# One transformer layer with retrieved experts in fp32: gates of the branches moved into the softmax pause, output projection by tiles, one-hot scaling on ScalarE

## The chip, the cores and the metric

The kernel runs on one core of one Trainium2 chip. The metric is the device time of one execution in microseconds (us). In the profile PE is TensorE's matmul, PEld its weight load, DVE is VectorE, ACT is ScalarE, POOL is GpSimd and SP is SyncE, which here only issues transfers. L740 is line 740 of the kernel before.

## What is computed

One layer on 512 tokens of width 1024, all in fp32. First half: a combined projection of x feeds a sliding-window attention (8 query heads, 2 key heads, chunks of 64 tokens, window of 2 chunks, sink logits) and a gated linear recurrence (4 heads, states of 128 x 128, chunks of 64). The two branches are projected to the width, weighted by sigmoid gates and sent through one output projection; then comes a layer norm. Second half: each token picks 128 of 16384 experts.

```python
mixed = (sigmoid(ga) * (attn @ w_proj_attn) + sigmoid(gh) * (rec @ w_proj_hgrn))
x = layer_norm(ALPHA * x + mixed @ w_out, ln1_g, ln1_b)
# peer_ffn: top 16 of 128 keys twice per head, top 16 of their sums, softmax g
hid = einsum('thkd,td->thk', u[e], xt)
act = gelu(hid)
out = einsum('thk,thkd->td', g * act, v[e])
x = layer_norm(ALPHA * x + out, ln2_g, ln2_b)
```

## The kernel before, in words

**Tiles.** The tokens are four tiles of 128. The first half of the layer runs twice: front A has tile 0, front B ("the big front") tiles 1 to 3, with six chunks. In the second half tiles 0 and 1 are GATHERED: GpSimd fetches single rows of u and v with indirect transfers (L1592), 512 KB for one expert slot of 128 tokens, into 12 slots. VectorE reduces each u row against x (L1163, rows 0 to 127 for tile 0 and 256 to 383 for tile 1) and adds each v row to an accumulator (L1178, rows 128 to 255 and 384 to 511). Tiles 2 and 3 are DENSE: TensorE computes the hidden values of all 16384 experts in 128 chunks (`hidden(c)`, L835), and ScalarE applies gelu (L1054). 96 of the chunks come first, the last 32 alternate with `combine(i)` (L860), which multiplies by v. The gates of the dense tiles are built as a matrix: VectorE compares indices with an iota (L1484) and scales the second half by the gate (L1486), four tokens at a time (a quad, 64 of them, two buffers). TensorE multiplies the two one-hots (`spread(q)`, L853), ScalarE copies the product (`copy_gates`, L1073), and every 8 quads it is stored to memory.

**Order.** Each engine's program is written out by hand and all waits are semaphores. VectorE's program is woven from the front's steps and the gathered rows: `rows_until(q)` works off rows until q of the 512 are done, and the positions stand in constants (AT_STATE, AT_REC, AT_MIX and so on). `rows_until(at_mix(m))` stands ahead of mix m: 90 rows for m = 0, then 95, 106, 111 and so on up to 143. In the output projection it stands ahead of the first three blocks of columns (152, 161, 170), then come EARLY_ROWS = 204, the routing of tiles 1, 2 and 3 with 7 or 8 rows each part, and `rows_until(2 * NE)`, 256, ahead of the one-hots. HOT_ROWS are spread over the quads.

**Front B on TensorE.** Projections of the features (L575) and of seven token items (L587, the first five early), scores, then the softmax. `turn_weights(c)` (L637) and `times_v(c)` (L652 to L659) make the attention of chunk c, L677 and L682 the recurrence's operands, `chunk_kv` (L696) and `tile_out` (L707, L711) its states and outputs. Then come four pairs of `gates(m), gates(m+1), branches(m), branches(m+1)` (L740, L750, L752). gates(m) for m >= 2 waits for mix m - 2, since it uses its banks. The output projection (L775) has 12 units of one tile and 256 columns, in four banks. VectorE takes each unit (L1343) and norms a tile after its last one (L1352 to L1363). The normed tiles are turned (L788) and projected to queries (L815).

**ScalarE in front B.** Exponentials of the softmax (L968), copies of the token items (L913), scaling of the softmax (L976), copies of the turned weights (L983) and of the attention (L991), kendT (L995), the recurrence's output (L1000), roots (L1003), recT (L1008), gate sigmoids (L1014). A function of another table is preceded by an ACT_TABLE_LOAD.

**Queues.** SP issues all loads in program order: weight items of 1 MB through a ring of three slots, each waiting for the item that its slot held; later u and v chunks. In the spread phase the loads of hidden weights run four chunks ahead, and the first gates are loaded behind the one for chunk 99. GpSimd's queue holds the gathers and, at its end, the stores of tiles 0 and 1.

```python
            for c in range(FIRST):
                if c == TURN_AT:
                    picks(0)
                    picks(1)
                if c == SPREAD_AT:
                    pe.wait_ge(pick_out, 2 * len(DENSE))
                hidden(c)
                for q in range(quads_by(c - 1), quads_by(c)):
                    spread(q)
```

Of the kernel before, what the change touches and what calls it, by code (L numbers as in the profile page):

```python
# [12 lines left out]
P = 128  # L13
# [34 lines left out]
RING, ITEMW = 3, 2048  # L48
# [29 lines left out]
EXP_AT = 49  # L78
TURN_AT = 51
SPREAD_AT, SPREAD_END = 52, 82  # L80
# [3 lines left out]
EARLY_ROWS, PAIR_ROWS, HALF_ROWS = 204, 7, 8  # L84
HOT_ROWS = 30
MID_ROWS = 314
# [4 lines left out]
ODD_STEP, AT_OUT, OUT_STEP, HGRN_STEP, STATE_STEP = 5, 152, 9, 3, 2  # L91
# [91 lines left out]
def build(nc, x, xT, w_items, keysT, pos, inv_freq, sinks, lb_logits, norm_g,  # L183
          ln1, ln2, ident_d, causal_d, chunk_d, iota_d, u_rows, v_rows, u_cols, v_cols, gates_d, act_d, out):
    with ExitStack() as ctx:
# [25 lines left out]
        ring = view(64, RING, ITEMW)  # L211
# [90 lines left out]
        hot_ready = sem("hot_ready")  # L302
        g_done = sem("g_done")
# [14 lines left out]
        out_done = [sem(f"out_done{k}") for k in range(2)]  # L318
# [36 lines left out]
        B.sig = view(152, 2, 2, B.n)  # L355
# [81 lines left out]
        def _(sp):  # L437
# [115 lines left out]
            for k in range(2):  # L553
                sp.wait_ge(out_done[k], 32)

        @block.tensor
        def _(pe):
# [3 lines left out]
            def front(F, other=None):  # L561
# [99 lines left out]

                pe.wait_ge(F.reached, V_ZERO)
# [60 lines left out]
                pe.wait_ge(F.proj_out, 2 * N_HQF + N_TOK * nt)  # L723
# [6 lines left out]

                def gates(m):
                    k = I_MIX + 3 * (m // 2) + m % 2
                    item_in(pe, F, k)
                    w = item(F, k).rearrange("p (c n) -> p c n", n=P)
                    if m >= 2:
                        pe.wait_ge(F.mix_out, m - 1)
                    b = 4 * (m % 2)
                    for g in range(2):
                        for c in range(KC):
                            last = mm(bank[:, b + g, 0:n], w[:, g * KC + c, :], F.act_in[:, c, :],  # L740
                                      start=c == 0, stop=c == KC - 1)
                    last.then_inc(F.gate_done, 1)
# [917 lines left out]
```

## Time and profile before

| | |
|---|---|
| median of 3 runs | 1645.16 us (1645.09 to 1646.64) |
| the profiled execution | 1645.0 us, its span 1643.2 us |
| mean granted TensorE clock | 0.964 |
| TensorE matmul busy | 1543.6 us, 94% |
| VectorE busy | 1131.2 us, 69% |
| ScalarE busy | 270.4 us, 16% |
| moved by transfers | 532.38 MB, mean 324 GB/s |

The times of the rows are counted from the start of the span. A busy TensorE is not TensorE at its peak: the ends of its matmuls are modelled. An fp32 matmul stands as two records, so a unit of 8 matmuls is "x16". A group's span in the timeline overlaps the next one's by the length of a matmul; the distance between two starts is the pace.

### The profile page before, as it was taken

To read this page: it belongs to the slowest core of one execution; us is meant where nothing else is said; L and a number is where in the kernel's file an instruction comes from. 1 tells how busy PE (TensorE), PEld (TensorE's weight loads), DVE (VectorE), ACT (ScalarE), POOL (GpSimd) and SP (SyncE) were. 2 spreads that over 40 slices of the span, in tenths; PEclk is the share of its full clock that TensorE was granted. 3 is DMA by queue.
4 is the path that set the end of the run, shared out by engine and by line. 5 is a ranking of instruction groups with operands and counts; after the bars stand their busy time and mean duration, and the time that the engine had idled before them with its cause. 6 is when DMAs were issued, how large, how long until landed. Compare 5 with 4: busy or idle time off the path is not lost.

```text
span 1643.2 us, 17974 instructions
## 1 busy us (share of the span) xinstructions
PE 1543.6 (94%) x6542; PEld 1098.7 (67%) x6542; DVE 1131.2 (69%) x2364; ACT 270.4 (16%) x543; POOL 610.0 (37%) x518
## 2 busy tenths in 40 slices
PE   8798999789998799999999999889999999999997
PEld 7697778665557566888888888756666544444443
DVE  1413899978769999999979999366556735545523
ACT  2601213621010111111134453100000000000000
POOL 0000543466667463322322223465534633424100
PEclk9898998779999799999999999989999999999999
DMA  7586967777999797998978878999999999999962
GB/s 297 203 275 212 397 228 265 251 246 273 412 398 374 275 403 282 316 330 288 327 255 312 319 277 299 410 383 405 404 408 406 405 402 380 395 393 392 369 218 77
DMA packets 145511, 532.38 MB, mean 324 GB/s; under 512 B 14864, under 2 KB 34064, under 8 KB 133904
## 3 DMA queue, kind: packets, MB, share of 16 engines
q0 software_dynamic: 74016, 269.52, 43.7%
q1 hardware_dynamic: 70256, 244.94, 40.0%
q10 hardware_dynamic: 1152, 16.78, 2.6%
q8 instruction: 52, 0.85, 0.2%
q14 instruction: 35, 0.29, 0.0%
HBM read 503.92 MB, written 27.26 MB: 323 GB/s over the span
## 4 chain that ended last, share of the span: by engine, by line
PE 74%; DVE 12%; DMA 7%; issue 3%; ACT 2%; POOL 0%; SPq 0%; DVEq 0%
PE bank L835 26%; PE bank L860 22%; PE bank L740 7%; PE bank L815 6%; PE bank L853 3%; DMA arena<-v_cols_d 3%; DVE arena L1163 2%; DMA arena<-gates_d 2%; DVE arena L1178 2%; PE bank L775 2%; PE bank L750 2%; PE bank L752 2%; PE bank L587 1%; PE bank L575 1%; DMA arena<-u_cols_d 1%
## 5 line engine op out<-in xcount | busy, mean ns | idle before, releaser
L1592 POOL DMA_INDIRECT arena<-u_d,arena x256 | 319.7, 1249 | 566.4 <-DVE arena L1163 315.9
L860 PE MATMUL bank<-arena 128*128 128x512 f32 x1024 | 448.2, 595 | 16.8 <-DVE arena L1501 14.1
L835 PE MATMUL bank<-arena 128*128 128x256 f32 x2048 | 452.9, 379 | 4.0 <-DMA arena<-u_cols_d 4.0
L835 PEld LDWEIGHTS bank<-arena 128*128 128x128 f32 x2048 | 386.6, 190 | 69.4 <-issue 17.8
L1592 POOL DMA_INDIRECT arena<-v_d,arena x256 | 288.9, 1129 | 362.9 <-DVE arena L1178 287.2
L860 PEld LDWEIGHTS bank<-arena 128*128 128x128 f32 x1024 | 195.1, 191 | 250.7 <-issue 227.2
L1178 DVE SCALAR_TENSOR_TENSOR arena<-arena 128x1024 f32<-128x1024 f32 x256 | 327.9, 1281 | 42.4 <-DMA arena<-v_d,arena 32.2
L1163 DVE CUSTOM_DVE_ANT_0 arena<-arena 128x1024 f32<-128x1024 f32 x256 | 304.2, 1221 | 68.5 <-DMA arena<-u_d,arena 67.9
L1501 DVE TENSOR_TENSOR arena<-arena 128x256 f32<-128x256 f32 x128 | 52.9, 420 | 159.5 <-DMA arena<-act_d 103.1
L1054 ACT ACTIVATE arena<-bank 128x256 f32<-128x256 f32 x128 | 49.2, 384 | 491.2 <-PE bank L835 491.1
L815 PE MATMUL bank<-arena 128*128 128x128 f32 (+1 forms) x512 | 118.9, 394 | 1.4 <-ACT arena L1021 1.4
L740 PE MATMUL bank<-arena 128*128 128x128 f32 (+1 forms) x512 | 113.9, 384 | 0.0
L815 PEld LDWEIGHTS bank<-arena 128*128 128x128 f32 x512 | 81.0, 200 | 35.8 <-issue 2.6
L587 PE MATMUL bank<-arena 128*128 128x256 f32 x448 | 100.0, 385 | 2.5 <-ACT arena L913 2.5
L740 PEld LDWEIGHTS bank<-arena 128*128 128x128 f32 x512 | 78.1, 192 | 34.8 <-issue 1.6
L587 PEld LDWEIGHTS bank<-arena 128*128 128x128 f32 x448 | 86.3, 193 | 15.5 <-ACT arena L913 2.9
L853 PE MATMUL bank<-arena 128*128 128x128 f32 x512 | 64.7, 278 | 5.5 <-DVE arena L1486 4.3
L1073 ACT ACTIVATE arena<-bank 128x512 f32<-128x512 f32 x64 | 65.3, 1083 | 21.9 <-PE bank L853 20.9
L853 PEld LDWEIGHTS bank<-arena 128*128 128x128 f32 x512 | 63.1, 191 | 8.6 <-DVE arena L1486 6.8
L775 PE MATMUL bank<-arena 128*128 128x256 f32 x256 | 60.4, 401 | 8.3 <-DVE arena L1333 5.9
L575 PE MATMUL bank<-arena 128*128 128x128 f32 (+1 forms) x256 | 58.5, 395 | 7.2 <-DMA arena<-w_items_d 7.2
L775 PEld LDWEIGHTS bank<-arena 128*128 128x128 f32 x256 | 51.5, 203 | 17.2 <-DVE arena L1333 6.7
(200 smaller groups left out, 1035.6 us busy)
## 6 DMA issues: line engine op xcount, KB each, us to landing
arena<-w_items_d SPq DMA_DIRECT2D x66, 1024.0 KB, 7.2
arena<-u_cols_d SPq DMA_DIRECT2D x128, 512.0 KB, 6.6
arena<-v_cols_d SPq DMA_DIRECT2D x128, 512.0 KB, 8.9
gates_d<-arena ACTq DMA_DIRECT2D x8, 2048.0 KB, 8.2
arena<-gates_d SPq DMA_DIRECT2D x16, 1024.0 KB, 16.7
act_d<-arena SPq DMA_DIRECT2D x8, 1024.0 KB, 9.3
arena<-act_d SPq DMA_DIRECT2D x8, 1024.0 KB, 16.7
arena<-u_d,arena POOLq DMA_INDIRECT x256, 8.7
```

Of the source, the lines that this page charges most:

```text
L575: last = mm(bank[:, b % 4, 0:n], w[:, c, b % 2 * P:(b % 2 + 1) * P], F.act_in[:, c, :], start=c == 0, stop=c == KC - 1)
L587: last = mm(bank[:, b % 4, 0:TW], F.act_in[:, c, t * P:(t + 1) * P], w[:, c, :], start=c == 0, stop=c == KC - 1)
L740: last = mm(bank[:, b + g, 0:n], w[:, g * KC + c, :], F.act_in[:, c, :], start=c == 0, stop=c == KC - 1)
L775: last = mm(bank[:, u % 4, 0:TW], F.mixT[:, c, t * P:(t + 1) * P], w[:, c, :], start=c == 0, stop=c == KC - 1)
L815: last = mm(bank[:, b % 4, 0:n], w[:, c, half * P:(half + 1) * P], F.act_in[:, c, :], start=c == 0, stop=c == KC - 1)
L835: last = mm(bank[:, 4 + c % 2, 0:ND], u_buf[:, c % UBUFS, k, :], B.act_in[:, k, B.n - ND:B.n], start=k == 0, stop=k == KC - 1)
L853: last = mm(bank[:, 6 + q % 2, j * NK:(j + 1) * NK], hot[:, q % 2, j, :], hot[:, q % 2, QUAD + j, :], start=True, stop=True)
L860: last = mm(bank[:, 2 * n + half, :], act_slot(i)[:, n * P:(n + 1) * P], v_buf[i % VBUFS][:, half * 512:(half + 1) * 512], start=i == 0, s ...
L1073: fn(stage[g % 2][:, :, k * QUAD:(k + 1) * QUAD].rearrange("p e t -> p t e"), bank[:, 6 + q % 2, :].rearrange("p (t e) -> p t e", t=QUAD), ...
L1163: v.tensor_tensor_reduce(rows[:, s, :], rows[:, s, :], x1[:, t, :], 1.0, 0.0, ALU.mult, ALU.add, hid[:, k:k + 1]).then_inc(row_used, 1)
L1178: v.scalar_tensor_tensor(out=acc[t], in0=rows[:, s, :], scalar=wv[:, k:k + 1], in1=acc[t], op0=ALU.mult, op1=ALU.add).then_inc(row_used, 1)
L1592: pool.indirect_dma_start(rows[:, r % SLOTS, :], None, table, bass.IndirectOffsetOnAxis(eidx[:, t, k:k + 1], 0)).then_inc(landed[r % SLOTS ...
```

## The change

Seven edits come together.

- **Gates in the pause.** In front B gates(0) and gates(1) are issued after the last token item, around the first two `turn_weights`, into banks 0 to 3 instead of 0, 1, 4, 5. Their sigmoids come on ScalarE after the kendT copies, and chunk_kv(0) waits for all four. B.sig gets a place of its own. ScalarE copies the last token item ahead of the softmax scaling.
- **Early part of the projection.** Six of the eight matmuls of units 0 and 1 are issued ahead of the last mix, in both fronts.
- **Units by tiles.** The order of units is tile by tile; VectorE's rows within the projection are only those up to 152.
- **Ring** of four slots.
- **One-hots.** The scaling by the gate goes from VectorE (one multiply per quad) to ScalarE (four activations of 128x128), ahead of the gelu of the same chunk, with a semaphore hot_scaled.
- **copy_gates** writes in the order of the stage and reads the bank with a stride.
- **Positions.** Everything at the picks and the spread is one chunk later; row quotas change. The stores of the gathered tiles are on SP's queue.

```diff
-RING, ITEMW = 3, 2048
+RING, ITEMW = 4, 2048
-EXP_AT = 49
-TURN_AT = 51
-SPREAD_AT, SPREAD_END = 52, 82
+EXP_AT = 50
+TURN_AT = 52
+SPREAD_AT, SPREAD_END = 53, 83
-EARLY_ROWS, PAIR_ROWS, HALF_ROWS = 204, 7, 8
-HOT_ROWS = 30
-MID_ROWS = 314
+EARLY_ROWS, PAIR_ROWS, HALF_ROWS = 184, 7, 7
+HOT_ROWS = 52
+MID_ROWS = 316
-        B.sig = view(152, 2, 2, B.n)
+        B.sig = view(48, 2, 2, B.n)
 def out_units(F):
-            return ([(k, t) for k in range(N_OUT - 2) for t in range(F.nt)]
-                    + [(k, t) for t in range(F.nt) for k in range(N_OUT - 2, N_OUT)])
+            return [(k, t) for t in range(F.nt) for k in range(N_OUT)]
+        def gate_bank(F, m):
+            return 2 * m if F is B and m < 2 else 4 * (m % 2)
 # SP, at the end
-            for n, t in enumerate(DENSE):
-                sp.wait_ge(y2_ready, len(GATHERED) + n + 1)
-                sp.dma_start(out[t * P:(t + 1) * P, :], x1[:, t, :]).then_inc(out_done[1], 16)
+            for n, t in enumerate(GATHERED + DENSE):
+                sp.wait_ge(y2_ready, n + 1)
+                sp.dma_start(out[t * P:(t + 1) * P, :], acc[t] if t in GATHERED else x1[:, t, :]).then_inc(out_done, 16)
 # TensorE
+                if F is B:
+                    gates(0)
                 pe.wait_ge(F.reached, V_ZERO)
                 turn_weights(0)
+                turn_weights(1)
+                if F is B:
+                    gates(1)
                 for c in range(F.nc):
-                    if c + 1 < F.nc:
+                    if 0 < c < F.nc - 1:
                         turn_weights(c + 1)
                     times_v(c)
...
-                pe.wait_ge(F.proj_out, 2 * N_HQF + N_TOK * nt)
+                if F is B:
+                    pe.wait_ge(F.gate_ready, 4)
+                else:
+                    pe.wait_ge(F.proj_out, 2 * N_HQF + N_TOK * nt)
                 chunk_kv(0)
...
+                pe.wait_ge(F.gate_ready, 2 * KC - 2)
+                pe.wait_ge(F.mix_out, KC - 2)
+                for u in range(2):
+                    item_in(pe, F, I_OUT + u)
+                    for c in range(KC - 2):
+                        sum_out(u, c)
                 pe.wait_ge(F.mix_out, KC)
...
 def spread(q):
-                pe.wait_ge(hot_ready, q + 1)
+                pe.wait_ge(hot_scaled, q + 1)
 # ScalarE
+                if F is B:
+                    for k in range(TOK_EARLY + 1, N_TOK):
+                        copy_tok(k)
                 for c in range(F.nc):
                     act.wait_ge(F.soft_den, c // (F.nc // 2) + 1)
...
-                for k in range(TOK_EARLY + 1, N_TOK):
-                    copy_tok(k)
+                if F is A:
+                    for k in range(TOK_EARLY + 1, N_TOK):
+                        copy_tok(k)
...
+                if F is B:
+                    gate_sigmoids(0)
+                    gate_sigmoids(1)
                 for t in range(nt):
                     act.wait_ge(F.o_done, t + 1)
...
+            def scale_hots(q):
+                act.wait_ge(hot_ready, q + 1)
+                for j in range(QUAD):
+                    d, t = divmod(q * QUAD + j, P)
+                    one = hot[:, q % 2, QUAD + j, :]
+                    last = fn(one, one, ACT.Copy, scale=gT[d][:, t:t + 1])
+                last.then_inc(hot_scaled, 1)
 def copy_gates(q):
-                fn(stage[g % 2][:, :, k * QUAD:(k + 1) * QUAD].rearrange("p e t -> p t e"),
-                   bank[:, 6 + q % 2, :].rearrange("p (t e) -> p t e", t=QUAD), ACT.Copy).then_inc(g_out, 1)
+                fn(stage[g % 2][:, :, k * QUAD:(k + 1) * QUAD],
+                   bank[:, 6 + q % 2, :].rearrange("p (t e) -> p e t", t=QUAD), ACT.Copy).then_inc(g_out, 1)
...
+                for q in range(quads_by(c - 1), quads_by(c)):
+                    scale_hots(q)
                 gelu(c)
                 for q in range(quads_by(c - 1), quads_by(c)):
                     copy_gates(q)
 # VectorE
-                    if t == 0 and k < N_OUT - 1:
-                        rows_until(AT_OUT + OUT_STEP * k)
+                    if u == 0:
+                        rows_until(AT_OUT)
...
-                    steps(lambda: v.tensor_tensor(out, iota..., idxT..., ALU.is_equal))
-                    v.tensor_tensor(out[:, 1, :, :], out[:, 1, :, :],
-                                    gT[d][:, ts]..., ALU.mult).then_inc(hot_ready, 1)
+                    v.tensor_tensor(out, iota..., idxT..., ALU.is_equal).then_inc(hot_ready, 1)
 # GpSimd, at the end
-            for t in GATHERED:
-                pool.wait_ge(y2_ready, t + 1)
-                pool.dma_start(out[t * P:(t + 1) * P, :], acc[t]).then_inc(out_done[0], 16)
```

## Rows read from the trace of the kernel before

**Rows 1.** The page's first part: busy us of each engine, share, instructions.
```profile
PE 1543.6 (94%) x6542; PEld 1098.7 (67%) x6542; DVE 1131.2 (69%) x2364; ACT 270.4 (16%) x543; POOL 610.0 (37%) x518
```

**Rows 2.** TensorE's waits: total us, times, longest.
```profile
PE bank L775 <- DVE arena L1333: 5.9, 2, 4.9
PE bank L853 <- DVE arena L1486: 4.3, 5, 1.2
```

**Rows 3.** Two stretches: length, busy us of each engine, granted clock, DMA share, GB/s.
```profile
320.00:334.00 14.00, 7.71 (x83) 6.12 (x85) 13.64 (x28) 10.67 (x30) 6.47 (x4) 0.53 0.71 246
840.00:1015.00 175.00, 169.55 (x1025) 154.91 (x1024) 156.94 (x195) 81.03 (x103) 39.31 (x29) 1.00 0.79 287
```

**Rows 4.** Timeline of TensorE, 300 to 345 us: start, length, line, [idle before].
```profile
310.02 7.17 PE L587 MATMUL bank<-arena 128*128 128x256 f32 x32 [2.53 <-ACT arena L913]
...
328.38 0.49 PE L656 MATMUL bank<-arena 128*64 128x64 f32 x4 [6.29 <-ACT arena L983]
...
342.64 1.71 PE L696 MATMUL bank<-arena 64*128 64x128 f32 x16
```

**Rows 5.** Timeline of ScalarE, 318 to 345 us.
```profile
318.47 7.12 ACT L976 ACTIVATE arena<-arena,mx 128x128 f32<-128x128 f32 x24 [3.77 <-DVE mx L1271]
325.61 1.28 ACT L913 ACT_TABLE_LOAD   x1
326.90 0.94 ACT L913 ACTIVATE arena<-bank 128x256 f32<-128x256 f32 x3
...
341.85 0.60 ACT L995 ACTIVATE arena<-bank 128x512 f32<-128x512 f32 x1 [0.73 <-PE bank L677]
```

**Rows 6.** The chain that ended last, the gate groups: start, us, what.
```profile
368.26 22.10 PE bank L740 x64
...
403.80 20.64 PE bank L740 x64
```

**Rows 7.** Timeline of VectorE, 375 to 400 us: first and last of 14 rows.
```profile
375.08 1.22 DVE L1163 CUSTOM_DVE_ANT_0 arena<-arena 128x1024 f32<-128x1024 f32 x1
...
389.98 1.22 DVE L1163 CUSTOM_DVE_ANT_0 arena<-arena 128x1024 f32<-128x1024 f32 x1
...
398.75 1.02 DVE L1331 TENSOR_TENSOR arena<-arena,bank 128x384 f32<-128x384 f32 x2 [7.54 <-PE bank L752]
```

**Rows 8.** Timeline of TensorE, 500 to 565 us.
```profile
501.57 37.61 PE L775 MATMUL bank<-arena 128*128 128x256 f32 x160 [4.89 <-DVE arena L1333]
...
563.03 13.39 PE L815 MATMUL bank<-arena 128*128 128x384 f32 x32 [0.69 <-ACT arena L1021]
```

**Rows 9.** Timeline of VectorE, 500 to 610 us: rows, a norm's start and the next tile's units.
```profile
501.43 12.39 DVE L1178 SCALAR_TENSOR_TENSOR arena<-arena 128x1024 f32<-128x1024 f32 x9
...
541.78 1.29 DVE L1352 BATCH_NORM_STATS2 stats<-arena 128x6 f32<-128x512 f32 x2
...
547.46 0.75 DVE L1343 SCALAR_TENSOR_TENSOR arena<-arena,bank 128x256 f32<-128x256 f32 x2
...
560.36 47.13 DVE L1178 SCALAR_TENSOR_TENSOR arena<-arena 128x1024 f32<-128x1024 f32 x34
```

**Rows 10.** Timeline of VectorE, 837 to 844 us: end of the picks, first quad.
```profile
837.61 0.29 DVE L1462 TENSOR_TENSOR arena<-arena 128x128 f32<-128x128 f32 x1
841.83 1.23 DVE L1484 TENSOR_TENSOR arena<-iota,chunk_mask 128x1024 f32<-128x1024 f32 x1 [3.93 <-ACT chunk_mask L1065]
843.09 0.69 DVE L1486 TENSOR_TENSOR arena<-arena,chunk_mask 128x512 f32<-128x512 f32 x1
```

**Rows 11.** Timeline of 848 to 854 us, TensorE and ScalarE: one chunk with two quads.
```profile
848.29 1.95 PE L853 MATMUL bank<-arena 128*128 128x128 f32 x16
849.38 1.99 ACT L1073 ACTIVATE arena<-bank 128x512 f32<-128x512 f32 x2 [0.51 <-PE bank L853]
850.07 3.62 PE L835 MATMUL bank<-arena 128*128 128x256 f32 x16
853.53 2.02 PE L853 MATMUL bank<-arena 128*128 128x128 f32 x16
```

More of the change, by code:

```diff
@@ L302, in build @@
         hot_ready = sem("hot_ready")
+        hot_scaled = sem("hot_scaled")
         g_done = sem("g_done")
@@ L317, in build @@
         y2_ready = sem("y2_ready")
-        out_done = [sem(f"out_done{k}") for k in range(2)]
+        out_done = sem("out_done")
         A.tok = view(0, 1, TOKW)
@@ L660, in times_v, with gates @@
                     last.then_inc(F.av_done, 1)
+                def gates(m):
+                    k = I_MIX + 3 * (m // 2) + m % 2
+                    item_in(pe, F, k)
+                    w = item(F, k).rearrange("p (c n) -> p c n", n=P)
+                    if m >= 2:
+                        pe.wait_ge(F.mix_out, m - 1)
+                    elif F is B:
+                        pe.wait_ge(F.proj_out, 2 * N_HQF + N_TOK * nt)
+                    b = gate_bank(F, m)
+                    for g in range(2):
+                        for c in range(KC):
+                            last = mm(bank[:, b + g, 0:n], w[:, g * KC + c, :], F.act_in[:, c, :],
+                                      start=c == 0, stop=c == KC - 1)
+                    last.then_inc(F.gate_done, 1)
+                if F is B:
+                    gates(0)
                 pe.wait_ge(F.reached, V_ZERO)
                 turn_weights(0)
+                turn_weights(1)
+                if F is B:
+                    gates(1)
                 for c in range(F.nc):
-                    if c + 1 < F.nc:
+                    if 0 < c < F.nc - 1:
                         turn_weights(c + 1)
@@ L728, in front @@
                     chunk_kv(2 * t + 2)
[L731 to L742, printed above, removed]
                 def branches(m):
@@ L770, in front @@
                     item_in(pe, F, I_OUT + k)
-                    w = item(F, I_OUT + k).rearrange("p (c n) -> p c n", c=KC)
                     if u >= 4:
                         pe.wait_ge(F.y_out, u - 3)
-                    for c in range(KC):
-                        last = mm(bank[:, u % 4, 0:TW], F.mixT[:, c, t * P:(t + 1) * P], w[:, c, :],
-                                  start=c == 0, stop=c == KC - 1)
+                    for c in range(KC - 2 if u < 2 else 0, KC):
+                        last = sum_out(u, c)
                     last.then_inc(F.y_done, 1)
@@ L996, in front, with gate_sigmoids @@
                        ACT.Copy).then_inc(F.kend_out, 1)
+                def gate_sigmoids(m):
+                    act.wait_ge(F.gate_done, m + 1)
+                    if m >= 2:
+                        act.wait_ge(F.mix_out, m - 1)
+                    for k in range(2):
+                        fn(F.sig[:, m % 2, k, :], bank[:, gate_bank(F, m) + k, 0:n], ACT.Sigmoid).then_inc(F.gate_ready, 1)
+                if F is B:
+                    gate_sigmoids(0)
+                    gate_sigmoids(1)
                 for t in range(nt):
@@ L1009, in front @@
                                ACT.Copy).then_inc(F.rec_out, 1)
[L1010 to L1014 removed]
+                    if m >= 2 or F is A:
+                        gate_sigmoids(m)
                     if F is B and m == GELU_M:
```

28 lines of the change are left out of this document (14 added, 14 removed).

## The prediction

> **What bounds the kernel now.** I read the page's first part, then the waits of TensorE, then the timelines of the stretches that the edits touch, engine by engine. TensorE is busy for 1543.6 of 1643.2 us [rows 1]: nearly all of the time is its matmuls, which the change neither adds nor removes, so it can only win some of the 100 us in which TensorE idles, or lose more. The waits [rows 2] show where edits can bite: the output projection waits for the last mix (L775, 5.9 us in two waits, one per front, the longest 4.9), and the spread for the one-hots (L853, 4.3 in five waits). The longest wait of all, that of the first combination of the dense part for its gates, the change doesn't reach: the gates are requested only behind the weight loads that wait for hidden(95), so the stall moves with the end of the spread phase. Behind TensorE stands VectorE: 156.9 of 175 us busy in the spread stage, ScalarE 81.0 [rows 3]. From 560.4 us to the first one-hot VectorE waits for almost nothing: it is as dense as TensorE.
>
> The profiled execution took 1645.0 us, its span 1643.2, the median of the runs 1645.16; the sum goes by 1645.0, and as the two agree within 0.2 us it stands for the median too. A difference of 0.2%, 3.3 us, is about what a measurement of this kernel can tell from none.
>
> **1. Front A.** Its projection begins six of eight summands of two units before the last mix. The wait it covers is the other L775 wait, 5.9 - 4.9 = 1.0 us [rows 2]. **-1.0**. A's new order of units is the old one (one tile), and its gates don't move.
>
> **2. Gates in the pause (front B).** TensorE finishes the last token item at 317.2, turns two chunks, and starts times_v at 328.4 [rows 4]. It idles since ScalarE scales until 325.6, loads a table and copies the last item's three tiles [rows 5]. The copies now come before the scaling; the last tile's can be done at about 317.7, and the scaling, which waits for VectorE until 318.5, isn't moved. One item of gates is half of 20.64 us, 10.3 [rows 6]. So gates(0) runs 317.7 to 328.1 and is hidden. Then two turns (1.1 at full clock) and gates(1), 10.3: times_v(0) starts at 339.5, not 328.4. The six chunks took 10.1 us from 328.4 to 338.5, partly at the half clock (0.53 granted over 320 to 334 [rows 3]); the odd and even chunks that ran at full clock give some 7.7 us for six, since TensorE now comes from dense work. They end at 347.2: +8.7. The turns and copies of the recurrence follow as before (ScalarE's last copy 342.45, now 351.2 [rows 5]). Here a wait is added: chunk_kv(0) needs the banks, so the four gate sigmoids: a table load and 4 x 0.44 us. The load took 1.29 us from the end of the scaling to the next activation [rows 5]. So 351.2 + 1.3 + 1.75 = 354.2, against 342.6 [rows 4]: **+11.6** for everything behind, VectorE's states and norms included. A low clock over chunk_kv adds about 1 (between 0 and 2): +12.6. The Trainium skill (ScalarE: Activation LUTs, What ACT_TABLE_LOAD costs) gives about 2.66 us for a switch of tables, its drain included; the row above shows 1.29, so the row decides, and by the page the wait would be 1.4 us longer.
>
> What is gained behind: 22.10 us of gates at 368.3 go [rows 6], so TensorE could start the branches soon after the norms. But gates(2) waits for mix(0), and VectorE owes 14 gathered rows ahead of it, whatever TensorE does: they ran from 375.1 to 391.1, 1.147 us each, and VectorE then waited 7.5 us for the branches [rows 7]. That slack of 7.5 us, and the 3.5 us between mix(0)'s end (400.3) and gates(2), are all that the delay can use up. The rows now end at 391.1 + 12.6 = 403.7, mix(0) takes 1.6, and gates(2) starts at 405.3, where it started at 403.8 [rows 6]: **+1.5**. TensorE idles some 5 us ahead of it and may find the half clock: between 0 and 3 us (half of a 6 us stretch), taken as **+1.6**. So 20 us of moved gates give nothing here: what is late next is VectorE's row quota, which isn't changed. The later pairs take TensorE 31 us, VectorE 16 rows and two mixes, 23 us, so they stay bound by TensorE.
>
> **3. Projection of front B.** Before: last mix done 501.5, matmuls 501.6 to 550, third norm's result at 560.3, query projection 563.0 [rows 8, 9]. After, with the same start: 24 of the records run in the 4.9 us wait; the first four units are done at about 510.2 (3.46 us each at full clock). VectorE does its nine rows until 513.8 [rows 9], so the fifth unit waits for a bank until 514.2. Eight units take 27.7: 541.9. VectorE finishes the first and second tile under these (1.5 us for four units, 5.7 for a norm [rows 9]); the third tile's norm ends at 541.9 + 0.4 + 5.9 = 548.2, against 560.3: -12.2. A half clock after the 4 us gap would cost up to 2.4; I take **-11.2**.
>
> The sum at this point: -1.0 + 1.5 + 1.6 - 11.2 = **-9.1**, for TensorE and VectorE alike.
>
> **4. From there to the spread.** Here the lead doesn't carry. VectorE did rows 152 to 170 within the projection; now it waits there. Before the first one-hot it had done 264 rows, now 256: the constants say 240, but rows_until(256) still stands ahead of the one-hots. From the third norm that is 104 rows of the second kind, instead of 86 of those and 8 of the first: +18 x 1.386 [rows 9] - 8 x 1.147 [rows 7] = +15.8. The picks used to be ready at 837.9 and the first one-hot waited 3.9 us for their way through TensorE and ScalarE [rows 10]; now 16 rows cover that way. First one-hot: 837.9 - 9.1 + 15.8 + 0.1 = 844.7, not 841.8. Then 1.3 for the comparison and 1.3 for ScalarE's four scalings (7.12 / 24 = 0.297 each [rows 5], plus start) instead of VectorE's 0.69 [rows 10]. The first spread starts at 847.4, against 848.3 [rows 11]: -0.9. TensorE has by then done one hidden chunk more (3.46): **-4.4** instead of -9.1. It waits some 4 us for the first pair of one-hots.
>
> **5. The spread phase.** Sixty-four quads in 30 chunks: 26 chunks with two, 4 with three. With two quads a chunk takes 3.46 + 1.8 = 5.26 us [rows 11]. ScalarE needs 0.38 + 2 x (1.19 + copy). The copy took 1.0 to 1.08 us where a plain 128x512 copy takes 0.60 [rows 11, 5]; its write now goes in runs of four words, its read from the bank is strided instead. At 0.6 ScalarE needs 4.0 us, at 1.08 4.9: under 5.26, so no stall. The removed multiplies (64 x 0.69 = 44 us) are VectorE's, which waited for TensorE here anyway: nothing. With three quads, the third one-hot waits for the first spread (two buffers). Before, the two spreads of 1.8 were followed by a stall of at most 1.2 [rows 2, 11]: its spread started some 3.1 us after the chunk's end. Now the chain is spread 0.9, comparison 1.3, scaling 1.3, and only then the gelu 0.35 and the copy of the first quad, for which the third spread waits as well, since the scaling of the third stands ahead of them on ScalarE: 1.1 + 1.27 + 1.3 + 0.35 + copy = 4.7 (copy 0.6) to 5.1 (copy 1.0). That is +1.6 to +2.0, four times; one of the four meets the sqrt root and its two table loads, +1.1 to +1.8 more; and the two smaller of the five waits now seen, 0.85 us together, go. In all **+6.6** (copy 0.6) to **+9.0** (copy 1.08). I take the lower end: the row nearest to a write in runs of four is the plain copy. The Trainium skill (SBUF — State Buffer, SBUF: two separate sides and the text on cachelines that follows) says that accesses staying in a 16-byte line run at full bandwidth, and that PSUM's lines are only 8 bytes, which it says of matmuls; no row here shows a strided bank read. By the first half the sum has the lower end, by the second the upper.
>
> **6. The rest.** Two fewer rows before the weights come in: hidden, as VectorE idles there. The stores of the gathered tiles go from GpSimd's queue to SP's, behind the last v load and still ahead of TensorE's end: nothing queues behind them but the two dense stores, which depend on later work. The fourth ring slot: TensorE's only wait for a weight item is the very first, so nothing; SP's load of x behind the turned recurrence is earlier with it. Each 0, within 1 us.
>
> **Sum:** -9.1 + 4.7 (part 4) + 6.6 = +2.2: **1647.2 us**.
>
> **The rivals.** *Faster:* the three-quad steps cost no more than now, because the comparison of the third quad is done early or ScalarE's order doesn't bite; then -4.4 stands, 1640.6 us. If besides VectorE reaches the first one-hot before 838, -9.1 stands, 1635.9. For: VectorE has 44 us less to do, and 13 us of waits of its own in the spread stage. Against: two one-hot buffers, and the row quota of 256. Chance 0.30. *Slower:* ScalarE saturates. It decides from a copy of about 1.25 us (0.38 + 2 x (1.19 + 1.25) = 5.26). At 1.35 each of 30 chunks is 0.2 longer, +6, and the stalls are +9.5 to +10: 1645 - 4.4 + 10 + 6 = 1656.6. Short of that, a copy of 1.08 (+9.0) with the half clock's 3 us at gates(2) and at the projection is 1645 - 4.4 + 9.0 + 2.6 = 1652.2; that is the value of this case. Chance 0.34. *The forecast*, no difference to be told, 0.36, own range 1643 to 1648.4. That moved gates save their whole 22 us is excluded by the row quota unless the recurrence isn't delayed by the pause.
>
> The range of 8 in 10 reaches from between the two faster values to beyond the slower one: **1638 to 1656**. Faster by over 0.2% (under 1641.9) 0.30, within 0.36, slower (over 1648.4) 0.34.
>
> **What would show it.** Gates(0) from about 318 at full clock; a table load and four sigmoids between the last kendT copy and chunk_kv(0), which starts near 353; VectorE without a wait before mix(0), and TensorE idle 3 to 6 us ahead of gates(2), that starts near 404 to 407; the third norm 9 us earlier; sixteen rows right before the first comparison, near 844, and TensorE waiting for it with one more chunk done; four waits of some 3 us each at L853's line; copy_gates at 0.6 or at 1.08 us. I am wrong if gates(2) starts before 400, if the first one-hot stands before 840, or if the waits of the spread are no longer than now.

## The result, and the profile after

The changed kernel takes **1666.29 us** (median of 4 runs, 1665.3 to 1668.73), the kernel before 1645.9 in the same comparison: ratio 1.0126, 95% interval 1.011 to 1.0142. It is slower by 20 us. The forecast was 1647.2 with a range to 1656: wrong in size and, as the likeliest case was no difference, in kind. The profiled execution took 1666.72 us, its span 1664.6 against 1643.2, **+21.4**; the mean granted clock is 0.955 (0.964 before). Three executions in a slow state, one of kernel 5 (2166.9 us) and two of kernel 9 (3269.7 and 2715.94 us), are left out of the medians below.

The page's first part, which answers to [rows 1]. The work is the same, and the span longer:

```profile
PE 1547.9 (93%) x6542; PEld 1102.6 (66%) x6542; DVE 1088.1 (65%) x2300; ACT 318.9 (19%) x800; POOL 588.4 (35%) x516
```

TensorE's waits (total us, times, longest), which answer to [rows 2]. L877 is the spread (L853 before), L884 the combination, L785 the output projection:

```profile
PE bank L884 <- DVE arena L1545: 19.0, 1, 19.0
PE bank L877 <- ACT arena L1108: 14.6, 1, 14.6
PE bank L877 <- ACT arena L1117: 11.7, 4, 4.0
...
PE bank L785 <- DVE arena L1389: 3.8, 1, 3.8
...
PE bank L719 <- ACT arena L1031: 2.7, 1, 2.7
```

Before, the spread waited 4.3 us for one-hots and 1.1 us for a copy of ScalarE, 5.4 in all; now it waits 26.3. The wait for the dense part's first gates grew from 13.6 to 19.0. Both lie behind 840 us. Up to there the forecast is close: within 0.2 us up to 354.3, within 1.3 us at the third norm. TensorE from the pause to the output projection:

```profile
317.61 10.56 PE L676 MATMUL bank<-arena 128*128 128x384 f32 x32 [0.56 <-ACT arena L937]
...
354.29 1.71 PE L719 MATMUL bank<-arena 64*128 64x128 f32 x16 [2.74 <-ACT arena L1031]
...
516.75 29.54 PE L785 MATMUL bank<-arena 128*128 128x256 f32 x128 [3.81 <-DVE arena L1389]
```

gates(0) starts at 317.61 (forecast 317.7), chunk_kv(0) at 354.29 (354.2) behind the sigmoids. In the chain, gates(2) and (3) stand so, where [rows 6] has 403.80 and 20.64:

```profile
404.53 22.36 PE bank L676 x64
```

Some 20 us of gates left this place, and still it begins 0.7 us later and lasts 1.7 us longer. VectorE's rows hold it, as forecast: TensorE waits 2.7 us there for mix 0. The third norm ends at 552.4 (forecast 551.2, before 560.3), 7.9 us earlier.

Now the place that failed. VectorE's timeline, 821 to 855 us:

```profile
821.48 0.28 DVE L1512 TENSOR_TENSOR arena<-arena 128x128 f32<-128x128 f32 x1
828.61 0.29 DVE L1506 TENSOR_REDUCE arena<-arena 128x8 f32<-128x128 f32 x1 [6.84 <-ACT arena L1094]
...
830.68 22.12 DVE L1224 SCALAR_TENSOR_TENSOR arena<-arena 128x1024 f32<-128x1024 f32 x16 [0.22 <-DVE arena L1508]
852.98 2.36 DVE L1530 TENSOR_TENSOR arena<-iota,chunk_mask 128x1024 f32<-128x1024 f32 x2 [0.18 <-DVE arena L1224]
```

and what held it, on ScalarE: the exponentials of the gates stand in its program behind the gelu of chunk 49 (EXP_AT is 50 now), and it waits for TensorE's chunks:

```profile
826.57 0.38 ACT L1089 ACTIVATE arena<-bank 128x256 f32<-128x256 f32 x1 [3.07 <-PE bank L859]
826.97 1.28 ACT L1094 ACT_TABLE_LOAD   x1
828.27 0.51 ACT L1094 ACTIVATE arena<-arena 128x128 f32<-128x128 f32 x2
```

VectorE stands for 6.84 us, then does the sixteen rows that the prediction counted, and the first comparison is at 852.98, not 844.7. In the kernel before, VectorE reached the same point (the arguments of the exponentials, L1466) at 835.46, behind the gelu of chunk 48, and waited 0.30 us:

```profile
835.46 0.29 DVE L1466 TENSOR_TENSOR arena<-arena 128x128 f32<-128x128 f32 x1
```

```profile
834.02 0.38 ACT L1054 ACTIVATE arena<-bank 128x256 f32<-128x256 f32 x1 [3.07 <-PE bank L835]
```

Back to the changed kernel: with the one-hots late, TensorE has no work that it may do:

```profile
835.66 5.34 PE L859 MATMUL bank<-arena 128*128 128x256 f32 x24
855.57 3.78 PE L877 MATMUL bank<-arena 128*128 128x128 f32 x16 [14.56 <-ACT arena L1108]
859.14 4.78 PE L859 MATMUL bank<-arena 128*128 128x256 f32 x16
...
899.72 1.13 PE L877 MATMUL bank<-arena 128*128 128x128 f32 x8 [2.58 <-ACT arena L1117]
...
988.76 2.04 PE L877 MATMUL bank<-arena 128*128 128x128 f32 x8 [3.96 <-ACT arena L1117]
```

Behind the 14.56 us the two spreads take 3.78 us where [rows 11] has 1.95, and the chunk 4.78 for 3.62; the granted clock over 855 to 860 us is 0.50, the lower of its two levels (1.2 GHz for 2.4), after those 14.56 us without a matmul. The lower two rows are each a third quad's spread, 1.13 us at full clock and 2.04 us at half clock (0.50 granted over 988 to 991 us). The whole phase in one row of a table by stretches, after and then before (columns as in [rows 3]):

```profile
855.00:1080.00 225.00, 212.43 (x1184) 192.92 (x1184) 148.04 (x191) 130.74 (x364) 70.40 (x62) 0.96 0.84 316
```

```profile
848.00:1062.00 214.00, 208.55 (x1202) 189.22 (x1201) 179.00 (x232) 84.48 (x110) 66.36 (x50) 1.00 0.83 308
```

TensorE idles 12.6 us of it (0.6 of them the end of the first spread's wait) against 5.5, and its busy time grows although it has one hidden chunk less to do. By the waits it stands for 11.7 us behind the first spread, where it stood for 5.4 before. Last, the chain of waits into the first combination:

```profile
1081.11 17.02 DMA arena<-gates_d
...
1098.22 0.43 DVE arena L1545
...
1098.70 6.24 PE bank L884 x8
```

Before, this load was issued at 1063.81 and took 11.61 us, and the combination began at 1076.00. The working for the span: chunk 95 ends 17.3 us later (the load's issue, 1081.11 - 1063.81), the load and what follows add 5.4, which makes 22.7 at the first combination, and the stretch behind it gives 1.3 back (waits of 2.3 us for 3.3, matmuls 0.3 less; no run tells which edit does it): 21.4.

### The profile page after: what moved, and what is told of

Read it like the earlier page. It is cut to its first block, busy times and chain, and to the rows that moved or that the text cites. A ratio compares the mean times of both kernels' runs of the same rounds, so it can differ in the third digit from the quotient of the medians.

```text
span 1664.6 us, 18169 instructions
## 1 busy us (share of the span) xinstructions
PE 1547.9 (93%) x6542; PEld 1102.6 (66%) x6542; DVE 1088.1 (65%) x2300; ACT 318.9 (19%) x800; POOL 588.4 (35%) x516
## 4 chain that ended last, share of the span: by engine, by line
PE 76%; DVE 12%; DMA 5%; issue 3%; ACT 3%; SPq 0%; POOL 0%; DVEq 0%
PE bank L859 26%; PE bank L884 24%; PE bank L676 7%; PE bank L839 6%; PE bank L877 4%; DVE arena L1209 3%; PE bank L785 3%; DVE arena L1224 2%; DMA arena<-v_cols_d 2%; PE bank L590 1%; PE bank L763 1%; PE bank L765 1%; DMA arena<-gates_d 1%; DMA arena<-u_d,arena 1%; DVE arena L1427 1%
## 5 line engine op out<-in xcount | busy, mean ns | idle before, releaser
L1636 POOL DMA_INDIRECT arena<-u_d,arena x256 | 304.5, 1189 | 516.4 <-DVE arena L1209 298.5
L884 PE MATMUL bank<-arena 128*128 128x512 f32 x1024 | 448.0, 595 | 21.3 <-DVE arena L1545 19.0
L1636 POOL DMA_INDIRECT arena<-v_d,arena x256 | 283.7, 1108 | 452.0 <-DVE arena L1224 380.8
L859 PEld LDWEIGHTS bank<-arena 128*128 128x128 f32 x2048 | 391.1, 192 | 67.0 <-issue 15.3
L884 PEld LDWEIGHTS bank<-arena 128*128 128x128 f32 x1024 | 195.5, 191 | 254.6 <-issue 228.4
L839 PEld LDWEIGHTS bank<-arena 128*128 128x128 f32 x512 | 81.4, 201 | 35.7 <-issue 2.7
L676 PEld LDWEIGHTS bank<-arena 128*128 128x128 f32 x512 | 78.2, 193 | 38.1 <-issue 5.6
L590 PEld LDWEIGHTS bank<-arena 128*128 128x128 f32 x448 | 87.4, 196 | 16.1 <-ACT arena L937 3.2
L877 PE MATMUL bank<-arena 128*128 128x128 f32 x512 | 67.5, 288 | 26.2 <-ACT arena L1108 14.6
L877 PEld LDWEIGHTS bank<-arena 128*128 128x128 f32 x512 | 66.1, 202 | 28.8 <-ACT arena L1108 23.2
L1530 DVE TENSOR_TENSOR arena<-iota,chunk_mask 128x1024 f32<-128x1024 f32 x32 | 38.3, 1223 | 36.8 <-PE bank L877 36.7
L785 PE MATMUL bank<-arena 128*128 128x256 f32 x256 | 57.5, 387 | 3.8 <-DVE arena L1389 3.8
```

The source lines that it names most:

```text
L590: last = mm(bank[:, b % 4, 0:TW], F.act_in[:, c, t * P:(t + 1) * P], w[:, c, :], start=c == 0, stop=c == KC - 1)
L785: return mm(bank[:, u % 4, 0:TW], F.mixT[:, c, t * P:(t + 1) * P], w[:, c, :], start=c == 0, stop=c == KC - 1)
L839: last = mm(bank[:, b % 4, 0:n], w[:, c, half * P:(half + 1) * P], F.act_in[:, c, :], start=c == 0, stop=c == KC - 1)
L859: last = mm(bank[:, 4 + c % 2, 0:ND], u_buf[:, c % UBUFS, k, :], B.act_in[:, k, B.n - ND:B.n], start=k == 0, stop=k == KC - 1)
L877: last = mm(bank[:, 6 + q % 2, j * NK:(j + 1) * NK], hot[:, q % 2, j, :], hot[:, q % 2, QUAD + j, :], start=True, stop=True)
L884: last = mm(bank[:, 2 * n + half, :], act_slot(i)[:, n * P:(n + 1) * P], v_buf[i % VBUFS][:, half * 512:(half + 1) * 512], start=i == 0, s ...
```

## The experiments

Twelve kernels ran; all compute the full output. Each ratio is to the kernel before, measured beside it (1644.5 us in these comparisons); "after" is 1666.3 us.

**1. Rows behind the first one-hots.** The sixteen rows leave the path to the spread.

```diff
-            rows_until(2 * NE)
-            dve.wait_ge(row_used, 2 * NE)
-            dve.wait_ge(ln_in, 64)
             dve.sem_inc(route_gate, 1)
             one_hots(0, first)
+            rows_until(2 * NE)
+            dve.wait_ge(row_used, 2 * NE)
+            dve.wait_ge(ln_in, 64)
```

> The changed kernel with the quota of 256 rows moved from ahead of the first one-hot to between the two halves of the one-hots, so that rows 240 to 256 are worked off among the first quads. Theory 1 (VectorE is late at the first one-hot, by 22 us for sixteen rows and 6.8 us for the wait on ScalarE's exponentials; TensorE's 14.6 us at the first spread and the half clock behind it, 3 us, are its price): the wait at the first spread falls from 14.6 to under 2 us, the time by 15 to 18, to about 1649. Theory 2 (ScalarE's order in the spread phase is what costs, and the first wait is only where it shows first): the wait goes but comes back at later spreads, and the time falls by less than 8 us.

1646.92 us, ratio 1.0014 (1.0003 to 1.0025): 19 us better than after. VectorE's first comparison:

```profile
834.39 2.36 DVE L1530 TENSOR_TENSOR arena<-iota,chunk_mask 128x1024 f32<-128x1024 f32 x2 [3.94 <-ACT chunk_mask L1100]
```

The spread's first wait is gone; the four for the third quads remain (11.7 us), and so does the long one for the gates (19.79). One call, kept ahead of the one-hots, is worth about as much as the whole loss. The recorded expectation was some 1649. This kernel takes the rows off TensorE's path and with them the wait for the exponentials; kernel 2 takes off the wait alone.

**2. Exponentials two chunks earlier.** 

```diff
-EXP_AT = 50
+EXP_AT = 48
```

> The changed kernel with ScalarE's exponentials of the gates at chunk 48 instead of 50. VectorE was ready for them at 821.8 us and got them at 828.6. Theory 1: VectorE goes on at about 824, everything up to the first one-hot is 4.5 us earlier, and so is the end: 1661 to 1662. If the first one-hot isn't bound by this chain, no change: 1666.

1659.17 us, 1.0093 (1.0076 to 1.011): -7, more than the 4.5 expected. The wait on the exponentials is gone and the rows start at 827.06, 3.6 us earlier, in an execution that was 3.4 us late from the queries on (558.49 for 555.13). The first spread waits 6.2 us less:

```profile
851.95 3.78 PE L877 MATMUL bank<-arena 128*128 128x128 f32 x16 [8.37 <-ACT arena L1108]
```

**3. Gates back behind the recurrence.** 

```diff
-            return 2 * m if F is B and m < 2 else 4 * (m % 2)
+            return 4 * (m % 2)
...
-                if F is B:
-                    gates(0)
                 pe.wait_ge(F.reached, V_ZERO)
                 turn_weights(0)
                 turn_weights(1)
-                if F is B:
-                    gates(1)
...
-                    pe.wait_ge(F.gate_ready, 4)
+                pe.wait_ge(F.proj_out, 2 * N_HQF + N_TOK * nt)
```

(their sigmoids go back too; the token copy stays ahead of the scaling).

> The changed kernel with gates(0) and gates(1) of the big front back behind the recurrence, in their old banks, their sigmoids in the old place; all else as changed. Theory 1 (VectorE's fourteen rows ahead of mix 0 set the start of gates(2) in both orders): gates(2) starts near 403, against 404.5, and the time is 0 to 3 us lower, 1663 to 1666. Rival (the move is worth the idle time that it fills, 8 us or more of the 20 moved): the time rises by 8 us or more, to 1674 or above.

1661.26 us, 1.0102 (1.0086 to 1.0119): -5, outside the 0 to 3 expected. chunk_kv(0) starts at 338.90, where the kernel before has 342.64 [rows 4]. Of these 3.7 us, 2.2 are the table load and the token copy that no longer stand behind the scaling (1.28 and 0.94 [rows 5]), and 0.75 is an earlier start of the scaling itself (317.72 for 318.47). The branches start at 389.01 and the chain has gates(2) at 399.60, 4.9 us before the changed kernel. So the moved gates cost 5 us; the rival, that they had saved something, falls.

**4. Two quads in every chunk.**

```diff
-SPREAD_AT, SPREAD_END = 53, 83
+SPREAD_AT, SPREAD_END = 53, 85
```

> The changed kernel with the 64 quads over 32 chunks instead of 30: two in each, never three. Theory 1: the four waits of 2.6 to 4.0 us (11.7 in all) at the third quads go, with the slow records behind two of them; no other wait grows; 1666 - 11 = 1655. If ScalarE is saturated in the steps of two quads as well, the waits come back elsewhere and less than 5 us are won.

1653.35 us, 1.005 (1.0033 to 1.0067): -13 (-11 expected). The third quads' waits are gone and no other takes their place in the spread; the first wait stays (14.5), and so do the first two spreads at half clock. The table by stretches shows TensorE busy throughout, at 0.99 of the clock (0.94 in the first 45 us, 1.00 behind them), and the chain what comes next:

```profile
855.00:1060.00 205.00, 204.63 (x1183) 186.87 (x1184) 145.14 (x187) 130.69 (x363) 68.48 (x57) 0.99 0.86 332
```

```profile
1061.98 22.62 DMA arena<-gates_d
```

The gates' load is issued 19.1 us earlier than after (1061.98 for 1081.11), 11.7 of it the waits and most of the other 7.4 the clock. The load, which now meets 5.61 MB of gathers while it runs (2.86 after), takes 5.6 us of it back.

**5. More rows within the spread** (on top of 1).

```diff
-HOT_ROWS = 52
+HOT_ROWS = 64
```

> e1_rows_in_hot with HOT_ROWS 64 instead of 52, so that 12 of the 24 rows behind the last quad are done among the quads. Theory (the first combination waits 19 to 20 us instead of 13.6 because the gathers of these rows are still moving when the first gates are loaded: in the kernel before VectorE's last such row ends 16 us ahead of that load, in e1 about 4): the wait falls to 13 to 15 us and the time by 5 to 6, to about 1641. Rival (the longer wait has another source, the stores of the gates or the v loads): the wait stays at 19 to 20 and the time as in e1, or higher by what the denser VectorE costs the spread.

1640.08 us, 0.9973 (0.9956 to 0.9989): 6.8 better than 1, near the 1641 expected. With the rows done earlier, GpSimd's gathers have run out before the gates are loaded. From the chain of waits and from TensorE's timeline:

```profile
1061.76 9.10 DMA arena<-gates_d
```

```profile
1071.43 3.78 PE L884 MATMUL bank<-arena 128*128 128x512 f32 x4 [11.10 <-DVE arena L1545]
```

The same load takes 9.10 us, where it took 17.79 in kernel 1 and 17.02 after. The gathers' queue (q0) in the 18 to 24 us around the load, in the three kernels after, before and this one:

```profile
q0 software_dynamic: 1071, 3.87, 40.5%
```

```profile
q0 software_dynamic: 540, 1.94, 24.3%
```

```profile
q0 software_dynamic: 1, 0.00, 0.0%
```

(packets, MB, share of 16 engines; 1077 to 1101, 1060 to 1080 and 1053 to 1071 us.) 3.87, 1.94 and 0 MB of gathers go with 17.0, 11.6 and 9.1 us.

**6. The four repairs together**: 1, 3, 4 and 5.

> e5_hot_64 with the gates of the pause back behind the recurrence (e3) and two quads in each of 32 chunks (e4). If the three causes are separate, their gains add: 1647 - 5 (gates' wait) - 5 (no gates in the pause) - 11 (third quads) = 1626, allowing 1624 to 1631, and both kernels are beaten. If they cover one another, it stays at 1635 or above.

1618.78 us, 0.9839 (0.9812 to 0.9866), below the 1624 to 1631 expected. The four steps came to 44 us one by one, and together they give 47.5: kernel 4 alone had lost 5.6 us of its gain to the gates' load, which takes 9.01 us here. This beats both kernels by 26 us and more; kernel 11 tells how much of that the seven edits hold together.

**7. The projection alone**, in the kernel before.

```diff
-RING, ITEMW = 3, 2048
+RING, ITEMW = 4, 2048
...
-            return ([(k, t) for k in range(N_OUT - 2) for t in range(F.nt)]
-                    + [(k, t) for t in range(F.nt) for k in range(N_OUT - 2, N_OUT)])
+            return [(k, t) for t in range(F.nt) for k in range(N_OUT)]
...
+                for u in range(2):
+                    item_in(pe, F, I_OUT + u)
+                    for c in range(KC - 2):
+                        sum_out(u, c)
                 pe.wait_ge(F.mix_out, KC)
...
-                    if t == 0 and k < N_OUT - 1:
-                        rows_until(AT_OUT + OUT_STEP * k)
+                    if u == 0:
+                        rows_until(AT_OUT)
```

> The kernel before with the projection's part of the change alone: ring of four, units tile by tile, six summands of two units early, VectorE's rows in the projection only up to 152; the row quotas (204, 8, 30, 314) and the one-hots stay. Theory 1 (the 18 rows that left the projection must be done before the picks): the third norm is 10 to 13 us earlier, the picks are ready 12 us later than before, TensorE waits at them for 15 to 25 us, and the time is 1653 to 1662. Rival (the projection's gain carries through, since VectorE catches up in the routing): 1634 to 1640.

1663.51 us, 1.0109 (1.0079 to 1.0139), just above the 1653 to 1662 expected. The queries start at 550.67 instead of 563.03 [rows 8], 12.4 us earlier, and at the picks TensorE gives back twice that:

```profile
855.57 0.90 PE L853 MATMUL bank<-ident,arena 128*128 128x128 f32 x3 [25.42 <-DVEq L1482]
```

Rows taken out of the projection reappear whole on the path to the picks: a faster stage made the kernel 19 us slower.

**8. Even quads in the kernel before.**

```diff
-SPREAD_AT, SPREAD_END = 52, 82
+SPREAD_AT, SPREAD_END = 52, 84
```

> The kernel before with the 64 quads over 32 chunks (52 to 84) instead of 30. The waits of 1.0 to 1.2 us at the third quads go, 4.3 us in four: 1640 to 1641. If VectorE, at 1.91 us a quad and half a row, can't hold the pace of two quads in a chunk, nothing changes.

1641.61 us, 0.9982 (0.9971 to 0.9993), -3 (1640 to 1641 expected). The spread's waits go, but the gates' wait is 18.9 for 13.6: even quads alone don't account for kernel 6.

**9. The scaling back on VectorE**, in kernel 6.

```diff
-                pe.wait_ge(hot_scaled, q + 1)
+                pe.wait_ge(hot_ready, q + 1)
...
-                for q in range(quads_by(c - 1), quads_by(c)):
-                    scale_hots(q)
...
+                    v.tensor_tensor(out[:, 1, :, :], out[:, 1, :, :],
+                                    gT[d][:, ts]..., ALU.mult).then_inc(hot_ready, 1)
```

> e6_combined with the scaling of the one-hots back on VectorE (one multiply of 0.69 us a quad), rows and all else as in e6. Theory: VectorE then needs 2 x (1.25 + 0.65 + a row of 1.15 to 1.39) = 6.1 to 6.6 us for a chunk that TensorE does in 5.24; e6 leaves VectorE 19.5 us of waits in the spread, so the time rises by 15 to 25 us, to 1634 to 1644. Rival (the scaling's place is free, as VectorE had waits of its own in the kernel before): within 5 us of e6.

1642.32 us, 0.9991 (0.9973 to 1.001): some 24 us slower than kernel 6, and 15 to 25 were expected. TensorE's waits have a new line on top:

```profile
PE bank L867 <- DVE arena L1516: 16.5, 29, 1.9
```

Over 835 to 1000 us VectorE is busy 161.9 of 165 us here, 147.0 in kernel 6, and TensorE 150.6 against 164.2.

**10. The old order of the gates' copy**, in kernel 6.

```diff
-                fn(stage[g % 2][:, :, k * QUAD:(k + 1) * QUAD],
-                   bank[:, 6 + q % 2, :].rearrange("p (t e) -> p e t", t=QUAD), ACT.Copy)
+                fn(stage[g % 2][:, :, k * QUAD:(k + 1) * QUAD].rearrange("p e t -> p t e"),
+                   bank[:, 6 + q % 2, :].rearrange("p (t e) -> p t e", t=QUAD), ACT.Copy)
```

> e6_combined with copy_gates as in the kernel before (bank read contiguously, stage written with a stride of 32 words). Its duration goes back from 0.60 to 1.0 to 1.1 us. Theory: ScalarE then needs 0.38 + 2 x (1.19 + 1.05) = 4.9 us of 5.24, and TensorE doesn't wait: 1619 to 1621. If ScalarE has no room, 5 us or more slower.

1617.98 us, 0.9834 (0.9816 to 0.9852): no difference from kernel 6. ScalarE's groups of this line, here and in kernel 6:

```profile
L1103 ACT ACTIVATE arena<-bank 128x512 f32<-128x512 f32 x64 | 64.5, 1095 | 4.9 <-PE bank L867 3.3
```

```profile
L1103 ACT ACTIVATE arena<-bank 128x512 f32<-128x512 f32 x64 | 38.1, 597 | 14.3 <-PE bank L867 13.5
```

With the new order ScalarE saves 26.4 us and waits more for TensorE in return. With two quads in a chunk it has the room.

**11. Both gates in the pause**, in kernel 6 (that is, kernel 5 with even quads).

> e6_combined with both gates in the pause, as the change has them. From e3 the pause gates cost 5 us at gates(2); theory: 1623 to 1625. Rival (that cost is covered by what follows): 1619.

1626.69 us, 0.9875 (0.9851 to 0.9898): 8 slower than kernel 6 (1623 to 1625 was expected). gates(2) starts at 405.78 instead of 400.37. TensorE's timeline has the first branches at half clock ahead of it (0.51 granted over 389.9 to 395 us, after a wait of 3.97 us for VectorE's norm), 5.27 us for eight records that take 2.74 in the next but one group:

```profile
389.93 5.27 PE L763 MATMUL bank<-arena 128*128 128x384 f32 x8 [0.69 <-ACT arena L1046]
...
397.62 2.74 PE L763 MATMUL bank<-arena 128*128 128x384 f32 x8
...
405.78 2.90 PE L676 MATMUL bank<-arena 128*128 128x384 f32 x4 [2.84 <-DVE arena L1379]
```

Even so TensorE waits 2.84 us more for mix 0, so VectorE and not the half clock sets the start. The gates' load takes another 2.5 us (11.49 for 9.01). All seven edits of the change are in this kernel, and only the places of VectorE's rows and of the quads differ: with its positions mended the change is worth 18 us over the kernel before, and the pause gates cost 8 of the 26 us of kernel 6.

**12. One gate in the pause**, in kernel 6: gates(0) alone, its two sigmoids right behind the scaling of the softmax.

```diff
+                if F is B:
+                    gates(0)
                 pe.wait_ge(F.reached, V_ZERO)
                 turn_weights(0)
                 turn_weights(1)
...
+                if F is B:
+                    gate_sigmoids(0)
                 copy_wT(0)
...
+                    pe.wait_ge(F.gate_ready, 2)
...
+                    if m or F is A:
+                        gates(m)
-                    gates(m)
                     gates(m + 1)
```

> e6_combined with gates(0) alone in the pause, its sigmoids right behind the scaling of the softmax (no table load ahead of chunk_kv), and gates(1) behind the recurrence. Theory: the pause holds 8 to 11 us of idle TensorE, and gates(0) needs 10.3, so times_v(0) starts 4 to 5 us later than in e6 while 10.3 us go from the stretch behind, where VectorE's fourteen rows leave 7 us: gates(2) starts near 394 to 396 instead of 400.4, the time is 1613 to 1616. Rival (no gates in the pause are worth anything, as the row quota sets the pace): 1618 or more.

1615.78 us, 0.9817 (0.9801 to 0.9833), the lowest and within the 1613 to 1616 expected, though its interval meets that of kernel 6. On ScalarE's timeline the table is loaded while gates(0) runs:

```profile
325.68 1.28 ACT L1017 ACT_TABLE_LOAD   x1
...
329.39 0.87 ACT L1017 ACTIVATE arena<-bank 128x384 f32<-128x384 f32 x2 [2.43 <-PE bank L676]
```

times_v(0) starts 5.8 us later than in kernel 6 (330.81 for 324.98), and gates(2) 6.7 us earlier (393.69 for 400.37); gates(3) then waits 2.57 us for mix 1, VectorE's rows again.

## Why the prediction was wrong, point by point

**Right.** Part 1: front A's wait is gone. Part 2: every start from 317.6 to 354.3 us within 0.2, and VectorE's rows as what is late next: gates(2) +0.7 and 1.7 longer, 2.4 in all for 3.1 forecast (TensorE idles 2.7 us there, for some 5 forecast). The sum took the moved gates for a loss, and kernels 3 and 11 show one, of 5 and 8 us. Part 3: 3.81 us of wait for 4 forecast; the third norm is 7.9 us earlier where the sum had 9.1, which is 1.2 us short. Part 5's place: four waits of 2.58, 2.57, 3.96 and 2.58 us, where "four waits of some 3 us" were named, with the copy at 0.60, the lower end taken. Part 6's stores and ring moved nothing that the trace shows, unless they are behind the 1.3 us given back at the end.

**The step that failed is part 4**, the way to the first one-hot. It said "First one-hot: 837.9 - 9.1 + 15.8 + 0.1 = 844.7". It is 852.98. The rows were counted right (16 in 22.12 us, and kernel 1 shows that they lie on the path). What the sum left out is a wait of VectorE for ScalarE. By the prediction's own numbers VectorE is through with the routing 22 us of rows and 2 us of normalising ahead of 844.7, near 820.7: it came there at 821.5. In the kernel before it came there at 835.5, 14.0 us later, since the sixteen rows stand behind this point now, not ahead of it. The exponentials that it needs come with TensorE's chunks, and these are only 10.9 us earlier (the gelu of chunk 48 at 823.12 for 834.02); by the diff they stand a chunk later besides (EXP_AT 49 to 50, 3.46 us). The 3.1 us and the 3.46 us make the wait, 6.84 for 0.30. The prediction has no term for that edit and none for a wait of VectorE for ScalarE ahead of the rows. The projection's shortfall makes the other 1.2. Kernel 2 takes the wait away. TensorE's balance at the first spread is 855.57 - 848.29 - 3.46 = +3.8 where I had -4.4: **8.2 us** of the miss. It idles 14.56 us for the 4 that I gave it: the whole 10.9 us by which its chunks were ahead, and 3.7 more.

**A term left out: the clock in part 5.** From the first spread to the end of chunk 95 the change loses 17.3 - 3.8 = 13.5 us, where I had +6.6: **6.9** of the miss. The stalls have the size that I gave them: waits of 11.7 for 5.4 us, +6.3. The other 7.2 us are matmuls at the lower clock, 0.96 granted for 1.00: the first pair and its chunk alone lose 3.0 (3.78 - 1.95 and 4.78 - 3.62), and a third quad's spread takes 2.04 for 1.13, with 5.60 for 3.62 in the chunk behind it. I had weighed the half clock at gates(2) and at the projection, and never at the spread, where the longest gaps arose. Kernel 4 shows both halves: no wait behind the first spread, and 0.99 granted.

**A statement that failed: the first paragraph.** "The longest wait of all ... the change doesn't reach ... the stall moves with the end of the spread phase." It grew by **5.4** us. VectorE's last u row ahead of the gates ends 8 us before the load is issued now, 16 us before it in the kernel before, and the gathers that these rows set free fall beside the load. What decides it is how many rows are left behind the last quad (20 before, 24 now, 12 in kernel 5) and how late that quad is (two chunks later in kernel 4, which has 24 rows too); part 6 passed over the quotas as hidden on VectorE; hidden on VectorE they were, but not on the transfers. Kernel 5 shows it. Over the time of the load alone the gathers move 0, 1.00, 2.86 and 5.61 MB in kernel 5, before, after and kernel 4, and it takes 9.1, 11.6, 17.0 and 22.6 us. The gathers aren't the only thing that counts: in kernel 11 they move 0.03 MB and the load takes 11.49 us, beside 4.22 MB of the other loads where kernel 6, at 9.01 us, has 3.20. What the order of packets within the queues does was not tested.

These three and the 1.3 us given back make 8.2 + 6.9 + 5.4 - 1.3 = 19.2, for the 19.1 us between forecast and median. None of the signs that the prediction named for being wrong came up (gates(2) before 400, the first one-hot before 840, waits of the spread no longer than before): all three look for a kernel faster than forecast, and the miss lay on the other side.

**The rivals.** The slower one, ScalarE saturated, had the right sign and the wrong mechanism: the copy took 0.60 us, and kernel 10 shows that 1.10 us costs nothing once the quads are even. Against the faster one I had the row quota of 256, and kernel 1 bears that out: without it the kernel comes level (1646.92, inside the range). Neither named the exponentials.

**Why did 44 us of removed multiplies bring nothing?** I said that VectorE waited for TensorE there anyway. The kernel before has such waits, 13.8 us of them for the spread; no kernel here moves the scaling alone in it. In kernel 9, with more rows placed in the spread, the same multiplies are worth 24 us. The Trainium skill (ScalarE: Activation LUTs, Rules for kernel authors) sends a multiplication to VectorE as the engine that does it faster, with a figure for bf16; for these fp32 tiles the rows agree (0.69 us for a quad on VectorE [rows 10], 2.44 for two quads on ScalarE), and kernel 9 shows that the slower engine wins by 24 us where the faster one is full.

## What to carry to other kernels

An engine that arrives earlier meets the next hand-placed wait: for each step that a change pulls forward, follow every semaphore it waits on to the position of its producer in the other engine's program, and ask in both directions who is late. Work taken out of one stage's shadow must be given a new place by name; in this kernel, moving 16 rows from ahead of the one-hots into the spread gave 19 us. When a change with several parts comes out at the wrong side, repair its constants before judging its parts: here the same seven edits went from a ratio of 1.0126 to 0.9875 (kernel 11), and to 0.9817 with one of the two gates out of the pause (kernel 12).

## What was not expected of the hardware

A copy of 128x512 that reads its bank with a stride of 512 bytes and writes runs of four words takes 597 ns, like one in plain order; one that reads in order and writes single words 128 bytes apart takes 1095. The Trainium skill (SBUF — State Buffer, Door 1: The DMA port swizzle) gives SBUF lines of 16 bytes, in which consecutive accesses run at full bandwidth, and PSUM lines of 8 bytes, whose cost it names for matmuls: its first half fits these two numbers, and for ScalarE the second shows no cost.

A switch of tables costs 1.28 us and 0.01 to 0.02 until the next activation (load at 351.31, activation at 352.60), and nothing where it stands ahead of a wait (load at 325.68 and activation at 329.39, behind 2.43 us of wait for TensorE, in kernel 12). The Trainium skill (ScalarE: Activation LUTs, What ACT_TABLE_LOAD costs) gives 2.66 us with a drain; no drain shows here.

A load of 1 MB took 9.1, 11.6, 17.0 or 22.6 us from issue to landing, with 0, 1.00, 2.86 and 5.61 MB of gathers moved beside it.
